# Two transformer blocks on one core: at five norms GpSimd adds the eighth chunk's squares, and TensorE's sums stand inside the second unit

## The chip, the cores and the metric

The kernel runs on one core of a Trainium2 chip. The metric is the device time of one execution in microseconds (us). The kernel before was timed three times: 914.53, 915.21 and 915.25 us, median 915.21 us.

## What is computed

Two stacked models run on 256 tokens of width 1024; the first adds 16 meta tokens in front, so most of its stages work on 272 columns. What matters here, cut from the reference:

```python
def rmsnorm(x, g):
    y = xf * lax.rsqrt(jnp.mean(xf * xf, axis=-1, keepdims=True) + NORM_EPS)
    return (y * g)

def conv_ffn(h, w_up, conv_w, conv_b, w_down):
    u = h @ w_up                       # 1024 -> 2 * 2816
    u = conv_b + sum(conv_w[j] * up[:, j:j + L] for j in range(3))
    gate, val = jnp.split(u, 2, axis=-1)
    return (jax.nn.silu(gate) * val) @ w_down

# first block, two layers: h += norm(mixer(norm(h))); h += norm(conv_ffn(norm(h)))
# second block: u = norm(h); proj = u @ w_in (gated linear attention and a convolution); h += mix @ w_out
#               u2 = norm(h); a, b = split(u2 @ w_gate_upffn); h += (silu(a) * b) @ w_down
#               u3 = norm(h); h += sigmoid(u3 @ w_ple_gate) * (p @ w_ple_proj); out = norm(h)
```

Every norm needs, for each token, the sum of 1024 squares before anything that was multiplied by it can be scaled.

## The kernel before, in words

Activations lie with their channels on the partitions: a tensor of 1024 channels is 8 chunks (DC = 8) of 128 channels x T tokens. All engine programs are written out by hand, one function for each engine (tensor, scalar, vector, gpsimd, and sync for the transfers), and meet through semaphores; each engine works its list in order. Nothing schedules them but the order in which the code stands.

**Weights.** A weight matrix is streamed in units. SP loads a unit into `raw`, ScalarE writes its rounded upper part `w_high`, VectorE (for some units with GpSimd, function `low`, L2031) writes the remainder `w_low` = raw - w_high. Two buffers of each alternate. TensorE makes three products for each 128x128 weight tile: high by high, low by high, high by low (L487 to L489, or L519, L520 and L525 where the first two are issued before the low part of the activation is there). An "up" unit has 16 tiles: 8 chunks of two blocks, so 48 products, each 256, 258 or 272 columns wide. The results of a unit stay in PSUM banks until VectorE takes them out, which also frees the banks; the unit after next uses the same banks.

**A norm.** The norm's gain is folded into the activation (`u_high`, `u_low`), and the factor 1/rms is applied to the results, since it is a factor of the token. So the first unit after a norm can be multiplied while the sum of squares is still being made. For the five norms of the change (named f0, f1, g, f2 and e: the three feed-forward "up" stages, the input projection of the second block, and the gate at the end) it goes like this:

- ScalarE writes `u_high` (L1094) and the squares of each chunk, into `m` (L1066, norms f0, f1, g) or into one of two buffers `sq` (L1076, norms f2 and e). VectorE writes `u_low` (L1455).
- GpSimd adds the squares of a chunk to `acc` (L2048, `add_square`), chunk after chunk, for chunks 0 to 6 (`range(DC - 1)`). For norms with squares in `m` it also waits for `u_low` of that chunk.
- TensorE multiplies the first unit, chunk after chunk as they come, and then issues `norm_sums`: for each of two or three token tiles a product of `acc` with a column of 1/1024 (L561), and the same for the squares of chunk 7 (L578, `last_sums`); both go into one PSUM bank. Each of these float32 products shows as two records in the trace.
- VectorE works nine small dependent steps on these sums (function `norm`, L1475 to L1493) and so has 1/rms of each token.
- TensorE spreads this over the partitions with `norm_rows` (L593), placed in the middle of the second unit: ahead of chunk 4 of 8.
- VectorE copies the rows (L1503) and from then on scales and takes out results (L1509).

At f0, f1 and g the second unit's `w_low` is made in two halves by VectorE at the very end of the stage before (L1546, `add_post`), after the last `u_low`. TensorE's second unit begins with a wait for the first half (`first_low`), and waits for the whole at chunk 4. At f2 and e it waits for the whole unit's parts at its start. At f2, GpSimd makes a quarter of each up unit's `w_low`.

The unit loop, where the change hangs its call (`between` is called ahead of the chunk of that number):

```python
                for at, k in enumerate(order or range(kc)):
                    ...
                    if middle is not None and at == kc // 2:
                        middle()
                    if first_low is not None and k * nb * P == first_half(n):
                        parts_ready(n)
                    if at in between:
                        between[at]()
```

Of the kernel before, what the change touches and what calls it, by code (L numbers as in the profile page):

```python
# [46 lines left out]
DC = D // P  # L47
# [35 lines left out]
BANKS = {"uv": UV_BANKS, "uk": UK_BANKS, "uqn": UQN_BANKS, "uqr": UQR_BANKS}  # L83
WO_BANKS = ((0, 2), (1, 3), (4, 5), (0, 2))
NORM_BANK, R_BANK = 6, 7

GUESS, GUESS_A, GUESS_B = 0x5F1FFFF9, 0.703952253, 2.38924456

# [131 lines left out]
def program(nc, dram, marks, final):  # L220
    ctx = ExitStack()
    with ctx:
# [8 lines left out]
        def done(name, i=None):  # L231


            engine, n, loop = marks.get(name, ("scalar", 1, None))
            stride = marks.get(("stride", engine, loop), 1)
            if final and name not in marks:
                raise KeyError(name)
            if isinstance(i, tuple):
                i, n = i[0], n - i[1] * stride
            return step_sems[engine], n if i is None else i * stride + n  # L240
# [24 lines left out]
        acc = sb("acc", [P, 2, 3 * P])  # L265
        sq = sb("sq", [P, 2, 3 * P])
# [200 lines left out]
        def _(pe):  # L467
# [26 lines left out]
            def unit(n, T, xs, chunk_ready=None, middle=None, i=None, order=None, first_low=None, between={}):  # L494

                U = UNITS[n]
                nb, kc = U["blocks"], U["tiles"] // U["blocks"]
                if first_low is not None:
                    pe.wait_ge(*done(first_low))
                elif n > 0:  # L500
                    parts_ready(n, i)
                for b in range(nb):
                    bank_free(U["first"] + b, i, 2 * nb)
                for at, k in enumerate(order or range(kc)):
                    high_ready, low_ready = chunk_ready if isinstance(chunk_ready, tuple) else (chunk_ready, None)
                    if high_ready is not None:
                        high_ready(k)
# [6 lines that stand above are left out]
                    out = [bank[BLOCKS[U["first"] + b]["bank"]][:, 0:T] for b in range(nb)]  # L514
                    if low_ready is not None:

                        for b in range(nb):
                            hi, lo = weights(n, k * nb + b)
                            nc.tensor.matmul(out[b], hi, xs[0][:, k, 0:T], start=at == 0, stop=False)  # L519
                            nc.tensor.matmul(out[b], lo, xs[0][:, k, 0:T], start=False, stop=False)  # L520
                        low_ready(k)
                    for b in range(nb):
                        hi, lo = weights(n, k * nb + b)
                        if low_ready is not None:
                            last = nc.tensor.matmul(out[b], hi, xs[1][:, k, 0:T], start=False, stop=at == kc - 1)  # L525
                        else:
                            last = three(out[b], hi, lo, xs[0][:, k, 0:T], xs[1][:, k, 0:T], at == 0, at == kc - 1)
                        if at == kc - 1:
                            last.then_inc(products, 1)
# [21 lines left out]
            def norm_sums(name, after, squares, last_chunk=False, over_what=None, late=(DC - 1,)):  # L551


                n, sums = len(squares), bank[NORM_BANK]
                what = over_what or [OVER_D] * n
                pe.wait_ge(*done(*after) if isinstance(after, tuple) else done(after))
                if over_what is not None:
                    nc.tensor.matmul(sums[:, 0:n], eps_w[:, :], ones[:, 0:n], start=True, stop=False,
                                     skip_group_check=True)
                for c, x in enumerate(squares):  # L560
                    last = nc.tensor.matmul(sums[0:x.shape[1], c:c + 1], x, over[:, what[c]:what[c] + 1],  # L561
                                            start=over_what is None and c == 0,
                                            stop=not last_chunk and c == n - 1, skip_group_check=True)
                for k in late if last_chunk else ():
                    if k == DC - 1:
                        last_sums(name, n)
                    else:
                        chunk_sums(name, n, k)
                if not last_chunk:
                    last.then_inc(*S.step(f"{name} sums"))  # L570
# [15 lines left out]
            def norm_rows(name, outs, first=0, signal=None):  # L586


                pe.wait_ge(*done(f"{name} inverse"))
                w = norm_height(name)  # L590
                for c, out in enumerate(outs):
                    unit_rows = ident if name in BY_SQRT else row_ident
                    last = nc.tensor.matmul(out, ny[0:w, first + c:first + c + 1].to_broadcast([w, P]),  # L593
                                            unit_rows[0:w, 0:out.shape[1]], start=True, stop=True)
                last.then_inc(*S.step(signal or f"{name} rows"))
# [25 lines left out]
            def token_rows(b, n, at=0):  # L621
                return [bank[b][:, at + t0:at + t0 + w] for t0, w in token_tiles(n)]
# [15 lines left out]
            def squares(a, n):  # L638
                return [acc[:, a, t0:t0 + w] for t0, w in token_tiles(n)]

            def ffn_up(l, T, sums_name):

                n0 = FIRST_UNIT[f"up{l}"]
                us = (uh, ul)
                unit(n0, T, us, high_then_low(sums_name))
                norm_sums(sums_name, f"{sums_name} acc {DC - 2}", squares(0, T), True)
                unit(n0 + 1, T, us, None, lambda: norm_rows(sums_name, token_rows(R_BANK, T)),
                     first_low=f"{sums_name} next low" if l < 2 else None)
                with pe.Fori(0, (FC - 2) // 2) as i:
                    for k in range(2):  # L650
                        unit(n0 + 2 + k, T, us, i=i)
# [296 lines left out]
            T = SEQ  # L948
            us = (uh, ul)
            unit(n, T, us, high_then_low("g"))  # L950
            norm_sums("g", f"g acc {DC - 2}", squares(0, T), True)
            unit(n + 1, T, us, None, lambda: norm_rows("g", token_rows(R_BANK, T)), first_low="g next low")
            pe.wait_ge(freed["v"], BLOCKS[FIRST_BLOCK["gin_a"]]["freed"])
            pe.wait_ge(tables_in, 16 * 6)
            for pair in range(2):
# [68 lines left out]
            ffn_down(2, T)  # L1024
            n = FIRST_UNIT["pgate"]
            unit(n, T, us, u_ready("e"))
            norm_sums("e", f"e acc {DC - 2}", squares(0, T), True)
            unit(n + 1, T, us, None, lambda: norm_rows("e", token_rows(R_BANK, T)))
            unit(n + 2, T, us)
            blocks_in_turn(n + 3, T, lambda b, k: (uh[:, k, 0:T], ul[:, k, 0:T]), DC,  # L1030
                           middle=lambda: norm_sums("out", f"out acc {DC - 5}", squares(0, T), True, late=()))
# [990 lines left out]
        def _(pool):  # L2022
# [16 lines left out]
            def add_square(name, c, T, ready, a=0, k=None):  # L2039
                label = c if k is None else k  # L2040
                pool.wait_ge(*ready)
                if name in SQUARES_IN_M and name != "out":

                    pool.wait_ge(*done(f"{name} u low {c}"))
                pool.wait_ge(*S.now())
                step = S.step(f"{name} acc {label}")
                x = m[:, c, 0:T] if name in SQUARES_IN_M else post1_square(c) if name == "post1" else sq[:, label % 2, 0:T]
                nc.gpsimd.tensor_tensor(acc[:, a, 0:T], acc[:, a, 0:T], x, ALU.add).then_inc(*step)  # L2048
# [35 lines left out]
                    add_square("post0", c, T1, done(f"post0 sq {c}"))  # L2084
                low(FIRST_UNIT["wo"] + u + 2)
            clear("post0")
            for c in range(DC - 1):
                add_square("f0", c, T1, done(f"f0 sq {c}"))
            up_lows(0)
            clear("f0")  # L2090
# [6 lines left out]
                add_square("post1", b, T1, done(f"post1 sq {b}"))  # L2097
            low(FIRST_UNIT["pool"] + 2)
            clear("post1")
            for c in range(DC - 1):  # L2100
                add_square("f1", c, SEQ + HISTORY, done(f"f1 sq {c}"))
            up_lows(1)
            clear("f1")
# [4 lines left out]
                nc.gpsimd.memset(t[:, :], 0.0).then_inc(*S.step())  # L2108
            nc.gpsimd.memset(Sd[:, :, :], 0.0).then_inc(*S.step("zeros"))
            clear("fpost1")  # L2110
            for c in range(DC - 1):
                add_square("g", c, T, done(f"g sq {c}"))
            for n in range(FIRST_UNIT["gin_a"] + 2, FIRST_UNIT["gin_c"] + 6):
                low(n)
            clear("g")
            for u in range(4):
                low(FIRST_UNIT["wout"] + u + 2)
                for c in range(2 * u, min(2 * u + 2, DC - 1)):
                    add_square("f2", c, T, done(f"f2 sq {c}"))
            low(FIRST_UNIT["pproj"] + 2)  # L2120
            up_lows(2)
# [7 lines left out]
                S.leave((DC - 2) // 2)  # L2129
            for c in range(DC - 2, DC):  # L2130
                low(n0 + c + 2)
                if c < DC - 1:
                    add_square("e", c, T, done(f"e sq {c}"))
            low(FIRST_UNIT["pgate"] + 2)
            low(FIRST_UNIT["pgate"] + 3)
            clear("e")
# [107 lines left out]
```

## Time and profile before

| | |
|---|---|
| median of 3 runs | 915.21 us (914.53 to 915.25) |
| the profiled execution's own time | 914.09 us |
| its span in the profile | 911.9 us |
| TensorE busy | 891.7 us, 98% of the span |
| VectorE busy | 680.7 us, 75% |
| ScalarE busy | 504.9 us, 55% |
| GpSimd busy | 180.9 us, 20% |
| chain that ended last | TensorE 87%, VectorE 7%, ScalarE 2% |
| mean granted TensorE clock | 0.994 |

The five norms stand at these times of the span: f0 at 143, f1 at 376, g at 577, f2 at 694 and e at 881 us. Their second units are where the timeline is to be read. A row of the timeline gives start, duration, engine, source line, operation, the tiles out<-in, and how many records are merged in it; in brackets stands idle time ahead of it and what ended it. Matmul records overlap each other, since they are pipelined: the pace is the distance between their starts.

### The profile page before, as it was taken

What the parts mean: (1) busy time and instruction counts of PE and PEld (TensorE: products, weight loads), DVE (VectorE), ACT (ScalarE), POOL (GpSimd) and SP (SyncE); (2) the same over time, 40 slices, a digit from 0 to 9 for tenths busy, and PEclk for the clock granted to TensorE, in tenths of its full rate; (3) what the DMA queues carried; (4) which work ended last, traced back from release to release, by engine and by line L of the source; (5) the groups of instructions that cost most, each with busy time, mean ns of one, the idle gap of its engine ahead of it and who ended that gap; (6) DMA issues with size and microseconds to landing.
All of it is one profiled execution on the core that took longest, in us unless ns stands there. A gap on an engine that the chain in (4) does not pass through costs nothing.

```text
span 911.9 us, 19861 instructions
## 1 busy us (share of the span) xinstructions
PE 891.7 (98%) x7330; PEld 868.3 (95%) x7330; DVE 680.7 (75%) x1174; ACT 504.9 (55%) x843; POOL 180.9 (20%) x165
## 2 busy tenths in 40 slices
PE   8999999999999998999999999999999999999997
PEld 8987889999999998999999999999999999999996
DVE  7767539999995427999999544889887888875556
ACT  6677656666664345666666535654465444444443
POOL 0029751000000014200000003100034333313312
PEclk9999999999999999999999999999999999999998
DMA  6652133544464530355555554333354555564431
GB/s 231 191 134 94 48 139 139 181 174 160 176 232 156 215 137 10 130 184 184 184 184 206 174 206 154 133 145 140 139 177 159 189 187 187 190 237 178 169 139 47
DMA packets 25731, 146.81 MB, mean 161 GB/s; under 512 B 3008, under 2 KB 9168, under 8 KB 10448
## 3 DMA queue, kind: packets, MB, share of 16 engines
q1 hardware_dynamic: 25680, 146.11, 45.4%
q8 instruction: 34, 0.56, 0.3%
q14 instruction: 17, 0.14, 0.0%
HBM read 142.82 MB, written 1.05 MB: 158 GB/s over the span
## 4 chain that ended last, share of the span: by engine, by line
PE 87%; DVE 7%; ACT 2%; DMA 1%; issue 1%; POOL 1%; SPq 0%; DVEq 0%; ACTq 0%; POOLq 0%
PE bank L487 25%; PE bank L488 25%; PE bank L489 24%; PE bank L746 2%; DVE u_low L1455 1%; PE bank L941 1%; DVE h L1535 1%; PE bank L762 1%; DVE bank L1527 1%; PE bank L593 1%; PE bank L780 1%; PE bank L578 1%; PE bank L525 1%; ACT w_high L1058 1%; DMA raw<-w_dq_dram 1%
## 5 line engine op out<-in xcount | busy, mean ns | idle before, releaser
L487 PE MATMUL bank<-u_high,w_high 128*128 128x256 f32 (+2 forms) x1328 | 379.2, 286 | 3.1 <-ACT m L1066 1.2
L488 PE MATMUL bank<-u_low,w_high 128*128 128x256 f32 (+2 forms) x1328 | 377.0, 284 | 0.0
L489 PE MATMUL bank<-u_high,w_low 128*128 128x256 f32 (+2 forms) x1328 | 375.8, 283 | 0.0
L1446 DVE TENSOR_TENSOR w_low<-raw,w_high 128x1024 fp32r<-128x1024 f32 (+6 forms) x112 | 190.7, 1702 | 101.6 <-ACT w_high L1058 100.5
L487 PEld LDWEIGHTS bank<-u_high,w_high 128*128 128x128 f32 x1328 | 250.8, 189 | 5.4 <-issue 1.3
L488 PEld LDWEIGHTS bank<-u_low,w_high 128*128 128x128 f32 x1328 | 250.4, 189 | 0.0
L489 PEld LDWEIGHTS bank<-u_high,w_low 128*128 128x128 f32 x1328 | 250.2, 188 | 0.0
L1058 ACT ACTIVATE w_high<-raw 128x1024 fp32r<-128x1024 f32 (+6 forms) x119 | 189.5, 1592 | 67.8 <-PE bank L489 60.4
L487 PE MATMUL bank<-x_high,w_high 128*128 128x256 f32 (+1 forms) x608 | 172.2, 283 | 0.3 <-DVE x_low L1886 0.3
L489 PE MATMUL bank<-x_high,w_low 128*128 128x256 f32 (+1 forms) x608 | 172.5, 284 | 0.0
L488 PE MATMUL bank<-x_low,w_high 128*128 128x256 f32 (+1 forms) x608 | 171.8, 283 | 0.0
L2048 POOL TENSOR_TENSOR acc<-acc,sq 128x256 f32<-128x256 f32 (+1 forms) x32 | 42.7, 1333 | 487.7 <-ACT sq L1076 486.7
L487 PEld LDWEIGHTS bank<-x_high,w_high 128*128 128x128 f32 x608 | 114.6, 188 | 0.7 <-issue 0.7
L488 PEld LDWEIGHTS bank<-x_low,w_high 128*128 128x128 f32 x608 | 114.5, 188 | 0.0
L489 PEld LDWEIGHTS bank<-x_high,w_low 128*128 128x128 f32 x608 | 114.3, 188 | 0.0
L1055 ACT ACTIVATE w_high<-raw 128x1024 fp32r<-128x1024 f32 (+2 forms) x68 | 69.6, 1023 | 71.1 <-PE bank L489 67.2
L2031 POOL TENSOR_TENSOR w_low<-raw,w_high 128x512 fp32r<-128x512 f32 (+1 forms) x29 | 64.3, 2216 | 140.4 <-ACT w_high L1058 140.4
L1440 DVE TENSOR_TENSOR w_low<-raw,w_high 128x1024 fp32r<-128x1024 f32 (+2 forms) x68 | 80.2, 1179 | 13.0 <-ACT w_high L1055 10.9
L1595 DVE SCALAR_TENSOR_TENSOR conv_out<-conv_in,par,conv_out 128x272 f32<-128x272 f32 (+1 forms) x176 | 79.1, 489 | 7.6 <-ACT conv_out L1128 2.0
L1509 DVE TENSOR_TENSOR conv_in<-bank,r_rows 128x256 f32<-128x256 f32 (+2 forms) x140 | 54.2, 427 | 15.7 <-PE bank L489 10.3
L1135 ACT ACTIVATE conv_out<-conv_out 128x272 f32<-128x272 f32 (+1 forms) x44 | 18.7, 425 | 73.7 <-DVE conv_out L1595 73.7
L1128 ACT ACTIVATE conv_out<-conv_in,par 128x272 f32<-128x272 f32 (+1 forms) x88 | 48.2, 595 | 9.6 <-DVE conv_in L1509 9.2
(236 smaller groups left out, 1101.3 us busy)
## 6 DMA issues: line engine op xcount, KB each, us to landing
raw<-w_up_dram SPq DMA_DIRECT2D x66, 1024.0 KB, 4.8
raw<-w_down_dram SPq DMA_DIRECT2D x24, 1408.0 KB, 6.0
raw<-w_gin_c_dram SPq DMA_DIRECT2D x4, 1536.0 KB, 6.6
raw<-w_wo_dram SPq DMA_DIRECT2D x4, 1024.0 KB, 5.6
raw<-w_wout_dram SPq DMA_DIRECT2D x4, 1024.0 KB, 4.9
raw<-w_pgate_dram SPq DMA_DIRECT2D x4, 1024.0 KB, 4.8
raw<-w_gin_v_dram SPq DMA_DIRECT2D x2, 1024.0 KB, 5.0
raw<-w_gin_g_dram SPq DMA_DIRECT2D x2, 1024.0 KB, 4.8
```

What stands on the lines that cost most here:

```text
L487: nc.tensor.matmul(out, hi, rhi, start=start, stop=False)
L488: nc.tensor.matmul(out, hi, rlo, start=False, stop=False)
L489: return nc.tensor.matmul(out, lo, rhi, start=False, stop=stop)
L1055: nc.scalar.activation(wh[n % 2][:, 0:split], raw[n % 2][:, 0:split], ACT.Copy).then_inc(*S.step(first))
L1058: nc.scalar.activation(wh[n % 2][:, split:cols], raw[n % 2][:, split:cols], ACT.Copy).then_inc(high_parts, 1)
L1128: nc.scalar.activation(cv[:, hf, 0:T], ur[:, hf, 2 + skip:2 + skip + T], ACT.Identity, bias=pcol(f"cb{l}", hf * FC + j), scale=pcol(f"cw{l ...
L1440: nc.vector.tensor_tensor(wl[n % 2][:, 0:split], raw[n % 2][:, 0:split], wh[n % 2][:, 0:split].bitcast(F32), ALU.subtract)\
L1446: nc.vector.tensor_tensor(wl[n % 2][:, split:cols], raw[n % 2][:, split:cols], wh[n % 2][:, split:cols].bitcast(F32), ALU.subtract).then_i ...
L1509: nc.vector.tensor_tensor(out, bank[BLOCKS[b]["bank"]][:, 0:T], rows[:, 0:T], ALU.mult)\
L1595: nc.vector.scalar_tensor_tensor(cv[:, hf, 0:T], ur[:, hf, skip + tap:skip + tap + T], pcol(f"cw{l}", (tap * 2 + hf) * FC + j), cv[:, hf, ...
L2031: nc.gpsimd.tensor_tensor(wl[n % 2][:, at], raw[n % 2][:, at], wh[n % 2][:, at].bitcast(F32), ALU.subtract).then_inc(low_parts_g, pool_cou ...
L2048: nc.gpsimd.tensor_tensor(acc[:, a, 0:T], acc[:, a, 0:T], x, ALU.add).then_inc(*step)
```

## The change

At the five norms GpSimd adds the squares of all eight chunks into `acc`. TensorE no longer multiplies the squares of chunk 7 by themselves; `norm_sums` is one group of two or three products, of `acc` alone. It moves from behind the first unit to the inside of the second, ahead of its third chunk (`SUMS_AT = 2`). It waits for GpSimd's eighth add. `norm_rows` stays ahead of the fifth chunk of the same unit. VectorE's and ScalarE's lists are unchanged.

```diff
+SUMS_AT = 2
...
                 unit(n0, T, us, high_then_low(sums_name))
-                norm_sums(sums_name, f"{sums_name} acc {DC - 2}", squares(0, T), True)
                 unit(n0 + 1, T, us, None, lambda: norm_rows(sums_name, token_rows(R_BANK, T)),
+                     between={SUMS_AT: lambda: norm_sums(sums_name, f"{sums_name} acc {DC - 1}", squares(0, T))},
                      first_low=f"{sums_name} next low" if l < 2 else None)
...
             unit(n, T, us, high_then_low("g"))
-            norm_sums("g", f"g acc {DC - 2}", squares(0, T), True)
-            unit(n + 1, T, us, None, lambda: norm_rows("g", token_rows(R_BANK, T)), first_low="g next low")
+            unit(n + 1, T, us, None, lambda: norm_rows("g", token_rows(R_BANK, T)), first_low="g next low",
+                 between={SUMS_AT: lambda: norm_sums("g", f"g acc {DC - 1}", squares(0, T))})
...
             unit(n, T, us, u_ready("e"))
-            norm_sums("e", f"e acc {DC - 2}", squares(0, T), True)
-            unit(n + 1, T, us, None, lambda: norm_rows("e", token_rows(R_BANK, T)))
+            unit(n + 1, T, us, None, lambda: norm_rows("e", token_rows(R_BANK, T)),
+                 between={SUMS_AT: lambda: norm_sums("e", f"e acc {DC - 1}", squares(0, T))})
...
-            for c in range(DC - 1):
+            for c in range(DC):
                 add_square("f0", c, T1, done(f"f0 sq {c}"))
...
-            for c in range(DC - 1):
+            for c in range(DC):
                 add_square("f1", c, SEQ + HISTORY, done(f"f1 sq {c}"))
...
-            for c in range(DC - 1):
+            for c in range(DC):
                 add_square("g", c, T, done(f"g sq {c}"))
...
                 low(FIRST_UNIT["wout"] + u + 2)
-                for c in range(2 * u, min(2 * u + 2, DC - 1)):
+                for c in range(2 * u, 2 * u + 2):
                     add_square("f2", c, T, done(f"f2 sq {c}"))
...
                 low(n0 + c + 2)
-                if c < DC - 1:
-                    add_square("e", c, T, done(f"e sq {c}"))
+                add_square("e", c, T, done(f"e sq {c}"))
```

On TensorE, norm f0, from the end of the first unit (L520 and L525) into the second (L487 to L489); before:

```order
L525 MATMUL bank<-u_low,w_high 128x272 x2
L561 MATMUL bank<-mean_weights,acc 91x1 x3
L578 MATMUL bank<-mean_weights,m 91x1 x3
L487 MATMUL bank<-u_high,w_high 128x272
L488 MATMUL bank<-u_low,w_high 128x272
L489 MATMUL bank<-u_high,w_low 128x272
```

And the change at the same place (its lines are numbered one higher), from the end of the second chunk of the second unit on, where the sums now stand:

```order
L488 MATMUL bank<-u_high,w_high 128x272
L489 MATMUL bank<-u_low,w_high 128x272
L490 MATMUL bank<-u_high,w_low 128x272
L562 MATMUL bank<-mean_weights,acc 91x1 x3
L488 MATMUL bank<-u_high,w_high 128x272
L489 MATMUL bank<-u_low,w_high 128x272
L490 MATMUL bank<-u_high,w_low 128x272
```

Twelve products of the second unit now stand ahead of the sums and twelve between them and the rows (L593, now L594), where 24 stood between sums and rows; the group on `m` is gone.

On GpSimd, norm f2, ahead of its share of the up units' `w_low`; before:

```order
L2031 TENSOR_TENSOR w_low<-raw,w_high 128x512
L2048 TENSOR_TENSOR acc<-acc,sq 128x256
L2031 TENSOR_TENSOR w_low<-raw,w_high 128x512
```

And in the change:

```order
L2032 TENSOR_TENSOR w_low<-raw,w_high 128x512
L2049 TENSOR_TENSOR acc<-acc,sq 128x256 x2
L2032 TENSOR_TENSOR w_low<-raw,w_high 128x512
```

One more add stands ahead of GpSimd's next share of `w_low`.

## Rows read from the trace of the kernel before

**Rows 1.** The page, part 1: busy time, share of the span, instructions.

```profile
PE 891.7 (98%) x7330; PEld 868.3 (95%) x7330; DVE 680.7 (75%) x1174; ACT 504.9 (55%) x843; POOL 180.9 (20%) x165
```

**Rows 2.** Timeline, TensorE, norm f0; columns as told in the section on the profile.

```profile
142.65 0.62 PE L578 MATMUL bank<-mean_weights,m 128*91 128x1 f32 x6
143.23 0.39 PE L487 MATMUL bank<-u_high,w_high 128*128 128x272 f32 x1
...
144.84 0.28 PE L487 MATMUL bank<-u_high,w_high 128*128 128x272 f32 x1
...
146.34 0.80 PE L593 MATMUL bank<-row_ident,norm_y 91*128 91x91 f32 x6
```

**Rows 3.** Timeline, VectorE, norm f0: first half of w_low, norm steps, taking out.

```profile
141.38 1.79 DVE L1546 TENSOR_TENSOR w_low<-raw,w_high 128x1024 fp32r<-128x1024 f32 x1
...
144.23 0.14 DVE L1475 TENSOR_SCALAR norm_t<-bank 91x3 int32<-91x3 int32 x1
...
145.76 0.16 DVE L1493 SCALAR_TENSOR_TENSOR norm_y<-norm_t,norm_y 91x3 f32<-91x3 f32 x1
...
148.63 0.79 DVE L1509 TENSOR_TENSOR conv_in<-bank,r_rows 128x272 f32<-128x272 f32 x2
```

**Rows 4.** Timeline, GpSimd, norm f0: the seventh add.

```profile
141.18 0.91 POOL L2048 TENSOR_TENSOR acc<-acc,m 128x272 f32<-128x272 f32 x1 [0.44 <-ACT m L1066]
```

**Rows 5.** Timeline, norm f1: second half of w_low, second unit's start, rows.

```profile
376.50 1.21 DVE L1546 TENSOR_TENSOR w_low<-raw,w_high 128x1024 fp32r<-128x1024 f32 x1
376.63 0.39 PE L487 MATMUL bank<-u_high,w_high 128*128 128x258 f32 x1
...
379.62 0.80 PE L593 MATMUL bank<-row_ident,norm_y 86*128 86x86 f32 x6
```

**Rows 6.** Timeline, norm g: first half of w_low, second unit's start, rows.

```profile
575.20 1.76 DVE L1546 TENSOR_TENSOR w_low<-raw,w_high 128x1024 fp32r<-128x1024 f32 x1
...
577.26 0.37 PE L487 MATMUL bank<-u_high,w_high 128*128 128x256 f32 x1
...
580.18 0.60 PE L593 MATMUL bank<-row_ident,norm_y 128*128 128x128 f32 x4
```

**Rows 7.** Timeline, norm f2: TensorE, VectorE's steps, GpSimd's share of w_low.

```profile
693.24 0.50 PE L561 MATMUL bank<-mean_weights,acc 128*128 128x1 f32 x4
693.60 0.58 PE L578 MATMUL bank<-mean_weights,sq 128*128 128x1 f32 x4
694.05 0.36 PE L487 MATMUL bank<-u_high,w_high 128*128 128x256 f32 x1
...
694.22 0.16 DVE L1475 TENSOR_SCALAR norm_t<-bank 128x2 int32<-128x2 int32 x1 [2.45 <-PE bank L578]
...
695.58 1.30 POOL L2031 TENSOR_TENSOR w_low<-raw,w_high 128x512 fp32r<-128x512 f32 x1 [2.66 <-ACT w_high L1058]
...
695.60 1.30 DVE L1491 SCALAR_TENSOR_TENSOR norm_t<-norm_t 128x2 f32<-128x2 f32 x1
...
697.15 0.71 PE L593 MATMUL bank<-row_ident,norm_y 128*128 128x128 f32 x4
```

**Rows 8.** Timeline, norm e: u_low of chunks 6 and 7, chunk 7, rows.

```profile
872.04 0.96 DVE L1455 SCALAR_TENSOR_TENSOR u_low<-h,par,u_high 128x256 fp32r<-128x256 f32 x1
...
879.84 0.48 DVE L1455 SCALAR_TENSOR_TENSOR u_low<-h,par,u_high 128x256 fp32r<-128x256 f32 x1
...
880.47 0.36 PE L487 MATMUL bank<-u_high,w_high 128*128 128x256 f32 x1
...
884.98 0.60 PE L593 MATMUL bank<-row_ident,norm_y 128*128 128x128 f32 x4
```

**Rows 9.** By source line, 668 to 671 us: two adds beside two u_low (min/median/max ns).

```profile
L2048 POOL TENSOR_TENSOR acc<-acc,sq x2: 742/1442/2143, 667.9 to 670.2; 128x256 f32<-128x256 f32 x2
...
L1455 DVE SCALAR_TENSOR_TENSOR u_low<-h,par,u_high x2: 958/963/968, 669.3 to 670.2; 128x256 fp32r<-128x256 f32 x2
```

**Rows 10.** TensorE in one stretch: length, busy, granted clock, DMA share, GB/s.

```profile
360.00:370.00 10.00, 8.55 (x59) 0.83 0.32 107
```

## The prediction

> **What bounds the kernel now.** I read the page first, for the shares: TensorE is busy for 98% of the span, VectorE for 75%, GpSimd for 20% [rows 1]. So a change pays only if it takes time from TensorE's list without making TensorE wait, and every new wait of TensorE is paid in full. Next I read the timeline at each of the five norms, TensorE beside VectorE and GpSimd. The reader is to see three things there.
>
> First, at f0 and f1 the second unit does not start when the sums are done but when the first half of its `w_low` is there. At f0 VectorE's first half runs from 141.38 for 1.79 us, to 143.17, and TensorE's first product stands at 143.23 [rows 2, 3]. At f1 the second half starts as the first ends, near 376.55, and TensorE starts at 376.63 [rows 5]. At g the first half ends at 576.96 and TensorE starts at 577.26, so there the sums held it [rows 6].
>
> Second, between sums and rows there are two chains side by side. TensorE's own 24 products take 3.11 us at f0 (143.23 to 146.34), 2.99 at f1 and 2.92 at g [rows 2, 5, 6]. VectorE's nine steps take 1.69 us at f0 (144.23 to 145.76 plus 0.16) [rows 3]; at f2 they take 2.87 us, of which 1.14 is one step that took 1.30 instead of 0.16, so 1.73 undisturbed [rows 7]. To this come 0.17 us from the first product behind the sums to the first step (694.05 to 694.22) and 0.06 from the last step (ending at 697.09) to the rows (697.15) [rows 7]. Today the 24 products cover this chain everywhere but at f2, where TensorE waits 0.2 us (24 products would end at 696.97).
>
> Third, VectorE and GpSimd take turns when both read SBUF. The first half at f0 takes 1.79 us where the same work takes 1.21 [rows 3, 5]; GpSimd's seventh add began just before it, at 141.18 [rows 4], and 141.18 + 1.21 + an add of some 0.77 is 143.16, the end seen. So they ran one after the other. At f2 the 1.30 us step starts 0.02 us behind a GpSimd `w_low` of 1.30 us and ends with it [rows 7].
>
> **What the change removes.** One group of small products at each norm: 0.36 us where it has four records (693.24 to 693.60) [rows 7]; with six I take 0.43 in proportion to the whole groups below. Together 2 x 0.43 + 3 x 0.36 = 1.94 us off TensorE's list. It is not all gained, since the unit that follows is held at f0, f1 and nearly at g.
>
> **What it adds and moves.** The remaining group costs 0.58 us with six records (142.65 to 143.23) and 0.45 with four (693.60 to 694.05) [rows 2, 7]. The group that is removed gives the lower bound, 0.43 and 0.36; I take the upper, because these are the rows in which TensorE goes from the sums back into a unit, as it now does. Behind the sums stand 12 products instead of 24: about 1.5 us. The chain needs 0.17 + 1.69 or 1.73 + 0.06 = 1.92 or 1.96 us. So TensorE waits about 0.45 us at the rows of every norm, whatever else happens. This is the core of the forecast: the wait alone eats what the removed group saves. Now each place.
>
> *f0.* The second unit still cannot start before 143.23. Twelve products end at 144.84 [rows 2]. GpSimd's eighth add can start when the seventh is through (142.09 by rows 4), finds VectorE in the first half, runs behind it until about 143.9 and pushes the second half to about 145.0; both are ready in time. Sums: 144.84 + 0.58 + 0.17 = 145.59 for the first step, rows at 145.59 + 1.69 + 0.06 = 147.34 instead of 146.34: **+1.00**.
>
> *f1.* 376.63 + 1.55 (half of 2.99, and 0.05 since the first half of such a run is the slower one) + 0.58 + 0.17 + 1.69 + 0.06 = 380.68 instead of 379.62: **+1.06**.
>
> *g.* The unit starts at 576.96 + 0.06 = 577.02. Then 1.51 + 0.45 + 0.17 + 1.73 + 0.06 gives 580.94 instead of 580.18: **+0.76** [rows 6].
>
> *f2.* Weights and squares are there early; the eighth add runs at about 688, in an idle time of VectorE, ahead of GpSimd's next `w_low`. The unit starts at 693.24, where the removed group stood. 1.41 (24 products without their slower start, halved) + 0.45 + 0.17: first step at 695.27, third step, the first that reads SBUF twice, at 695.66. But GpSimd's `w_low` runs from 695.58 to 696.88 [rows 7], triggered by ScalarE's work on the next weights, which does not move. Today it meets the eighth step; now it meets the third, which ends at 696.90, and six more steps of 0.195 end at 698.07. Rows at 698.13 instead of 697.15: **+0.98**. If they miss each other the rows stand at 697.08, 0.07 earlier; I take the meeting, because the third or, at the latest, the fifth step falls into those 1.30 us.
>
> *e.* The eighth add is new beside `u_low` of chunk 7. For chunk 6 there is an add, and its `u_low` takes 0.96 us; for chunk 7 there is none, and it takes 0.48 [rows 8]. TensorE takes up chunk 7 at 880.47, right behind this `u_low` (880.32). So chunk 7 comes 0.48 later. Then, from the end of the first unit, 1.41 + 0.45 + 0.17 + 1.73 + 0.06 = 3.82 us to the rows, where now 0.81 + 2.92 = 3.73 pass: **+0.57**. If the add does not get in, +0.09.
>
> The sum is 1.00 + 1.06 + 0.76 + 0.98 + 0.57 = **4.37 us**. Behind the rows everything is the same work. VectorE's list shifts a little more than TensorE's at f0 (its last step from 145.92 to 147.28, 1.36 against 1.00); it then has to take out the first unit's results, today until 149.42 [rows 3], before the third unit can start near 150.0 (the rows' 0.6 and 24 products of 3.1 after 146.34). That margin of 0.6 shrinks to 0.2 and holds. Nothing later waits for anything but TensorE's progress, so I let the 4.37 pass through. The profiled execution took 914.09 us, 1.12 less than the median; 914.09 + 4.37 = 918.46, and against the median 915.21 + 4.37 = **919.6 us**.
>
> **A rule against the row.** Who wins when the eighth add and the waiting first half meet? The row: of two adds in a row beside two waiting `u_low`, the first add held off the first `u_low`, then that `u_low` ran (969 ns until 670.3), and the second add, from 670.2, held off the second [rows 9]. They alternate, so at f0 the first half keeps its end at 143.17. The Trainium skill ("SBUF — State Buffer", section "Who interferes with whom") says that a VectorE instruction with two SBUF inputs and a GpSimd instruction that reads SBUF exclude each other for a whole instruction, and that issue order decides. By that rule too the first half, issued at 141.38, goes ahead of the add; if instead the add were counted first, the first rival below would be the sum. The same rule speaks against the change as such: it puts five more GpSimd instructions beside VectorE's most urgent work.
>
> **Rivals.** *The add goes first.* GpSimd's eighth add follows its seventh at once and VectorE's first half waits for both. The first half at f0, f1 and g then ends about 0.75 us later (1.79 - 1.21 = 0.58 was the part of one add that it met; a whole undisturbed one is 742 ns [rows 9]), and TensorE's second unit with it: + 2.25, in all 6.6 us, 921.8. For it: the first half shows that a GpSimd instruction in flight is never broken off. Against it: rows 9. Chance 0.10.
>
> *The clock falls.* At f2 TensorE will wait some 1.6 us (from 695.10 + 1.41 to 698.13). The one stretch in mid-span where the granted clock is below 1 follows a wait and small sums of similar size: 8.55 us busy in 10, granted 0.83 [rows 10], which is 1.7 us lost at the lower of the two levels (1.2 GHz). That would give 6.1 us, 921.3. Against it: at f2 twelve full products lie between sums and wait. Chance 0.05.
>
> *The chain fits (not slower).* If rows were never waited for, because the sums reach VectorE sooner than 0.17 us or its steps run closer, what is left is TensorE's own list: at f0 and f1, where the start is held anyway, +0.58 each; at g -0.24 + 0.45; at f2 and e -0.36 each. That is +0.65 us, 915.9. It decides at a chain of 1.5 us from sums to rows, against 1.92 in the rows. Against it: nine dependent steps at a distance of 0.19 have one length. Chance 0.07. If beyond that the first halves did not hold the second unit, the whole 1.94 us would be gained, 913.3; chance 0.03.
>
> **How the numbers follow.** A measurement of this kernel can tell about 0.2%, 1.8 us, from no change. My forecast, 0.75, with its bounds: sums at their lower costs -0.57, f2 without the meeting -1.05, e without the collision -0.48, which leaves 2.27 us and 917.5. That is still over 0.2%. Upwards the rivals of the add and of the clock reach 921.8. So the range is 917.5 to 921.9, faster 0.03, within 0.2% 0.07, slower 0.90.
>
> **What would show it.** TensorE idle ahead of the rows at all five norms, released by VectorE's last step: about 0.45 us at four, 1.6 at f2. The second unit of f0 and f1 starting as long after the last `u_low` as today. The second half of `w_low` at f0, f1 and g taking 1.9 instead of 1.21 us (if it is the first half that grows, the first rival holds). `u_low` of chunk 7 at e taking 0.96. I am wrong if the rows are reached without a wait, or if the time is under 917.

## The result, and the profile after

The changed kernel takes 918.78 us (median of 6 runs, 917.84 to 919.36) against 915.11 us before (6 runs). The ratio is 1.0044, with a 95% interval of 1.0034 to 1.0054: slower by some 4 us. The forecast was 919.6 us.

The page's first part of the kernel after:

```profile
PE 891.4 (97%) x7306; PEld 866.8 (95%) x7306; DVE 682.6 (74%) x1174; ACT 504.7 (55%) x843; POOL 188.3 (21%) x170
```

The 24 records fewer on TensorE (12 products in two records each) took nothing off its busy time that one would see, and the span grew from 911.9 to 916.4 us. So the time went into waits: TensorE's idle time grew from 20.2 to 25.0 us. The first two rows of TensorE's waits in the kernel after, longest in total first (columns: us in total, times, longest); the lines are numbered one higher than before:

```profile
PE bank L594 <- DVE norm_y L1494: 2.1, 5, 1.1
PE bank L488 <- DVE w_low L1547: 2.1, 3, 0.9
```

Neither row was in the list before. The first is the wait for VectorE's last norm step, at all five norms. The second is the wait for the first half of `w_low` at f0, f1 and g, which the sums had covered.

**Where the time went, norm by norm.** The same few waits of TensorE occur in both traces between the norms, so their starts serve as marks. Timeline of the kernel before (the fence holds TensorE's rows; ScalarE's `u_high` of chunk 7 at e, the mark between f2 and e, has a fence of its own):

```profile
141.11 0.51 PE L525 MATMUL bank<-u_low,w_high 128*128 128x272 f32 x2 [0.19 <-DVE u_low L1455]
341.69 0.33 PE L865 MATMUL bank<-w_high,u_high 128*96 128x256 f32 x1 [0.36 <-ACT u_high L1094]
374.55 0.51 PE L525 MATMUL bank<-u_low,w_high 128*128 128x258 f32 x2 [0.17 <-DVE u_low L1455]
566.88 0.36 PE L519 MATMUL bank<-u_high,w_high 128*128 128x256 f32 x1 [0.22 <-ACT u_high L1094]
664.13 0.36 PE L487 MATMUL bank<-x_high,w_high 128*128 128x256 f32 x1 [0.30 <-DVE x_low L1886]
903.28 0.77 PE L578 MATMUL bank<-mean_weights,m 128*128 128x1 f32 x4 [0.69 <-ACT m L1066]
```

```profile
877.51 0.49 ACT L1094 ACTIVATE u_high<-h,par 128x256 fp32r<-128x256 f32 x1
```

The same marks in the kernel after:

```profile
140.80 0.52 PE L526 MATMUL bank<-u_low,w_high 128*128 128x272 f32 x2 [0.20 <-DVE u_low L1456]
342.38 0.33 PE L866 MATMUL bank<-w_high,u_high 128*96 128x256 f32 x1 [0.36 <-ACT u_high L1095]
376.46 0.51 PE L526 MATMUL bank<-u_low,w_high 128*128 128x258 f32 x2 [0.18 <-DVE u_low L1456]
569.83 0.36 PE L520 MATMUL bank<-u_high,w_high 128*128 128x256 f32 x1 [0.22 <-ACT u_high L1095]
667.86 0.36 PE L488 MATMUL bank<-x_high,w_high 128*128 128x256 f32 x1 [0.29 <-DVE x_low L1887]
908.16 0.61 PE L579 MATMUL bank<-mean_weights,m 128*128 128x1 f32 x4 [0.69 <-ACT m L1067]
```

```profile
881.79 0.49 ACT L1095 ACTIVATE u_high<-h,par 128x256 fp32r<-128x256 f32 x1
```

After minus before, from mark to mark: f0 (-0.31 to +0.69) is +1.00 us; f1 (+1.91 to +2.95) +1.04; g (to +3.73) +0.78; f2 (to +4.28) +0.55; e (to +4.88) +0.60. Together **3.97 us**. Between f0 and f1 the trace after lost another 1.22 us, from +0.69 to +1.91. It is left out of the sum; the last section says what is known of it.

**Norm f0 in the kernel after.** TensorE, then VectorE, then GpSimd (the two halves of `w_low` in rows of their own):

```profile
142.93 0.39 PE L488 MATMUL bank<-u_high,w_high 128*128 128x272 f32 x1 [0.87 <-DVE w_low L1547]
...
144.53 0.57 PE L562 MATMUL bank<-mean_weights,acc 128*91 128x1 f32 x6
144.96 0.37 PE L488 MATMUL bank<-u_high,w_high 128*128 128x272 f32 x1
...
146.91 0.90 PE L594 MATMUL bank<-row_ident,norm_y 91*128 91x91 f32 x6 [0.19 <-DVE norm_y L1494]
147.60 0.38 PE L488 MATMUL bank<-u_high,w_high 128*128 128x272 f32 x1
```

```profile
141.09 1.79 DVE L1547 TENSOR_TENSOR w_low<-raw,w_high 128x1024 fp32r<-128x1024 f32 x1
142.80 1.78 DVE L1547 TENSOR_TENSOR w_low<-raw,w_high 128x1024 fp32r<-128x1024 f32 x1
...
145.14 0.16 DVE L1476 TENSOR_SCALAR norm_t<-bank 91x3 int32<-91x3 int32 x1 [0.56 <-PE bank L562]
...
146.70 0.16 DVE L1494 SCALAR_TENSOR_TENSOR norm_y<-norm_t,norm_y 91x3 f32<-91x3 f32 x1
```

```profile
140.88 0.91 POOL L2049 TENSOR_TENSOR acc<-acc,m 128x272 f32<-128x272 f32 x1 [0.43 <-ACT m L1067]
141.96 1.53 POOL L2049 TENSOR_TENSOR acc<-acc,m 128x272 f32<-128x272 f32 x1 [0.17 <-POOL acc L2049]
```

The unit starts 1.84 us after the first half began, as before (143.23 - 141.38 = 1.85, [rows 2, 3]): it was held by that half then, and it is now, only that now the trace shows the wait of 0.87 us. The first half keeps its 1.79 us; the second takes 1.78 us, where 1.21 stood before [rows 5]. The eighth add, issued at 141.96, lasts 1.53 us, twice its usual 0.77: it lets the first half finish, and the second half waits for it. VectorE's first step comes 0.61 us behind the start of the sums, the last ends at 146.86, and the rows follow at once. The group of rows then takes 0.69 us to the next product (146.91 to 147.60), where it took 0.59 before:

```profile
146.93 0.37 PE L487 MATMUL bank<-u_high,w_high 128*128 128x272 f32 x1
```

### The profile page after: what moved, and what is told of

Same layout as the page of the kernel before. It is cut to its first block, busy times and chain, and to the rows that moved or that the text cites. A ratio compares the mean times of both kernels' runs of the same rounds, so it can differ in the third digit from the quotient of the medians.

```text
span 916.4 us, 19823 instructions
## 1 busy us (share of the span) xinstructions
PE 891.4 (97%) x7306; PEld 866.8 (95%) x7306; DVE 682.6 (74%) x1174; ACT 504.7 (55%) x843; POOL 188.3 (21%) x170
## 4 chain that ended last, share of the span: by engine, by line
PE 84%; DVE 11%; ACT 2%; issue 1%; DMA 1%; POOL 1%; SPq 0%; DVEq 0%; POOLq 0%; ACTq 0%
PE bank L488 24%; PE bank L489 24%; PE bank L490 24%; DVE u_low L1456 2%; PE bank L747 2%; DVE h L1536 1%; DVE bank L1528 1%; PE bank L594 1%; PE bank L942 1%; PE bank L763 1%; DVE w_low L1447 1%; PE bank L781 1%; ACT w_high L1059 1%; PE bank L562 1%; PE bank L579 1%
## 5 line engine op out<-in xcount | busy, mean ns | idle before, releaser
L489 PE MATMUL bank<-u_low,w_high 128*128 128x256 f32 (+2 forms) x1328 | 377.1, 284 | 0.0
L489 PEld LDWEIGHTS bank<-u_low,w_high 128*128 128x128 f32 x1328 | 250.5, 189 | 0.0
L489 PE MATMUL bank<-x_low,w_high 128*128 128x256 f32 (+1 forms) x608 | 171.8, 283 | 0.0
L2049 POOL TENSOR_TENSOR acc<-acc,sq 128x256 f32<-128x256 f32 (+1 forms) x34 | 45.5, 1338 | 490.4 <-ACT sq L1077 489.2
L489 PEld LDWEIGHTS bank<-x_low,w_high 128*128 128x128 f32 x608 | 114.5, 188 | 0.0
```

The lines of the kernel that those rows point to most:

```text
L489: nc.tensor.matmul(out, hi, rlo, start=False, stop=False)
```

## The experiments

Theory 1 is the forecast's: the place of the sums costs, since 12 products do not cover VectorE's steps, and the saved group is worth nothing where the unit waits for `w_low`. Theory 2: GpSimd's five added adds cost, by holding VectorE. Theory 3: a longer stretch of low clock makes part of the difference. For each kernel the ratio of its time to the kernel before's is given, and the shifts at the five norms against the profile before, from mark to mark as above (one profile of each kernel, read to 0.01 us).

| kernel | f0 | f1 | g | f2 | e | sum | ratio, 95% interval |
|---|---|---|---|---|---|---|---|
| the change | +1.00 | +1.04 | +0.78 | +0.55 | +0.60 | +3.97 | 1.0044 (1.0034 to 1.0054) |
| sums ahead of the second chunk | +0.51 | +0.49 | +0.26 | -0.05 | +0.02 | +1.23 | 1.0011 (1.0002 to 1.0021) |
| place only | +1.49 | +1.49 | +1.28 | +1.13 | +0.55 | +5.94 | 1.0066 (1.0050 to 1.0081) |
| adds only | +1.14 | +1.10 | +0.82 | -0.55 | +0.01 | +2.52 | 1.0047 (1.0031 to 1.0063) |
| rows two chunks later | +0.86 | +1.04 | +3.19 | +0.51 | +0.58 | +6.18 | 1.0048 (1.0032 to 1.0064) |
| late add at e | +1.00 | +1.01 | +0.81 | +0.55 | +0.11 | +3.48 | 1.0045 (1.0028 to 1.0062) |
| f2 and e only | +0.04 | -0.01 | 0.00 | -0.55 | -0.42 | -0.94 | 0.9996 (0.9987 to 1.0005) |

### The sums one chunk earlier

```diff
-SUMS_AT = 2
+SUMS_AT = 1
```

> The change with the sums one chunk earlier in the second unit (ahead of its second chunk instead of its third). Theory 1 (the place costs: with 12 products between sums and rows VectorE's nine steps are not covered): 18 products, some 2.2 us, cover 1.95 us, so TensorE has no wait at the rows at f0, f1, g and e, at most 0.1 at f2. What is left against before: f0 and f1 +0.5 each (the unit is held by the first half of w_low, and the group now stands behind it), g +0.2, f2 0, e +0.1 (u_low +0.48, group -0.36). Sum +1.3 to +1.5 us, 916.5 us. Theory 2 (the five added GpSimd adds cost, by holding VectorE): they are all still there, so nothing is won, 918.5 to 919. Theory 3 (part of the difference is the longer stretch of low clock between f0 and f1, not the norms): the norms' sum in the trace is then unlike the time's difference.

Measured: 915.82 us (median of 11 runs) beside 914.96. Norm f0 on TensorE in this kernel:

```profile
142.98 0.39 PE L488 MATMUL bank<-u_high,w_high 128*128 128x272 f32 x1 [0.86 <-DVE w_low L1547]
...
143.84 0.57 PE L562 MATMUL bank<-mean_weights,acc 128*91 128x1 f32 x6
...
146.59 0.80 PE L594 MATMUL bank<-row_ident,norm_y 91*128 91x91 f32 x6
```

There is no wait ahead of the rows at four norms. At f2 there are 0.48 us, where at most 0.1 was expected: VectorE's eighth step still meets GpSimd's `w_low` and takes 1.04 instead of 0.16 us. All five adds are there, and so is the wait for the first half; what is left at f0 is 0.51 us: the group that now stands behind that wait (0.43, from 143.84 to the next product at 144.27) and the slower start of that product. One chunk more between sums and rows brings back 2.7 of the 4.0 us. Theory 2 expected nothing to come back.

### The place alone

```diff
-            for c in range(DC):
+            for c in range(DC - 1):
                 add_square("f0", c, T1, done(f"f0 sq {c}"))
...
-                     between={SUMS_AT: lambda: norm_sums(sums_name, f"{sums_name} acc {DC - 1}", squares(0, T))},
+                     between={SUMS_AT: lambda: norm_sums(sums_name, f"{sums_name} acc {DC - 2}", squares(0, T), True)},
```

(against the change, and so at all five norms)

> The place alone: seven adds and both groups as before, moved together ahead of the third chunk of the second unit. Theory 1: rows later by 1.5 us at f0 and f1, 1.1 at g, 1.0 at f2, 0.5 at e (no new add beside u_low, so that one stays at 0.48 us). Sum +5.1 us, 920.2 us; TensorE waits about 0.45 us ahead of the rows at four norms. Theory 2: without the adds there is no loss; below 916.5 us. In both the second half of w_low at f0, f1 and g is back at 1.21 us.

Measured: 920.9 us. Without a single added add the kernel is slower than the change. So theory 2 falls as the account of the loss; what the adds cost at single places, two experiments below tell. In the trace the second half of `w_low` at f0 is back at its own duration, and so is `u_low` of chunk 7 at e:

```profile
143.02 1.21 DVE L1547 TENSOR_TENSOR w_low<-raw,w_high 128x1024 fp32r<-128x1024 f32 x1
```

```profile
885.66 0.48 DVE L1456 SCALAR_TENSOR_TENSOR u_low<-h,par,u_high 128x256 fp32r<-128x256 f32 x1
```

The difference to the change at f0, 0.49 us, is the second group, now in the path of the sums. Place by place 1.5, 1.5, 1.1, 1.0 and 0.5 us were expected and 1.49, 1.49, 1.28, 1.13 and 0.55 found. (The places expected add up to 5.6; the 5.1 given with them was added wrongly.)

### The adds alone

```diff
                 unit(n0, T, us, high_then_low(sums_name))
-                norm_sums(sums_name, f"{sums_name} acc {DC - 2}", squares(0, T), True)
+                norm_sums(sums_name, f"{sums_name} acc {DC - 1}", squares(0, T))
```

(against the kernel before, at all five norms, with GpSimd's list as in the change)

> The adds alone: eight adds, one group of sums, but behind the first unit, where the sums were before. Theory 1: no wait ahead of the rows anywhere (24 products in between), but TensorE waits for the eighth add at f0, f1 and g, since that runs behind the first half of w_low: +1.0, +1.1, +0.7 us. At f2 the group is saved and VectorE's steps end before GpSimd's w_low starts: -0.5. At e +0.1. Sum +2.4 us, 917.5 us. Theory 2 expects about as much as the change, +3.7 us, 918.8, since all five adds are there.

Measured: 918.54 us from 4 runs that lie far apart (916.38 to 920.95); the profiled one is the fastest. Theory 1 expected 917.5 and theory 2 918.8, so the time alone does not tell them apart; the norms in the trace do. They give +2.52 us. The interval of the ratio does not reach down to that; the other runs lost more than the profiled one, and their granted clock was lower (0.989 in the slowest, 0.994 in the profiled). The last 1.0 us between 917.5 and 918.54 has no cause shown. The norms themselves came as expected: 1.14, 1.10 and 0.82 us at f0, f1 and g (1.0, 1.1 and 0.7 expected), -0.55 at f2 and nothing at e, and no wait ahead of the rows anywhere. At f0 TensorE and GpSimd:

```profile
143.76 0.64 PE L561 MATMUL bank<-mean_weights,acc 128*91 128x1 f32 x6 [1.48 <-POOL acc L2048]
```

```profile
142.17 1.53 POOL L2048 TENSOR_TENSOR acc<-acc,m 128x272 f32<-128x272 f32 x1 [0.17 <-POOL acc L2048]
```

So the adds do cost at f0, f1 and g when TensorE needs the sum right behind the first unit: the eighth add stands behind VectorE's first half. The change had hidden this cost inside the second unit and paid for hiding it.

### The rows two chunks later

```diff
-SUMS_AT = 2
+SUMS_AT, ROWS_AT = 2, 6
...
-                unit(n0 + 1, T, us, None, lambda: norm_rows(sums_name, token_rows(R_BANK, T)),
-                     between={SUMS_AT: lambda: norm_sums(sums_name, f"{sums_name} acc {DC - 1}", squares(0, T))},
+                unit(n0 + 1, T, us,
+                     between={SUMS_AT: lambda: norm_sums(sums_name, f"{sums_name} acc {DC - 1}", squares(0, T)),
+                              ROWS_AT: lambda: norm_rows(sums_name, token_rows(R_BANK, T))},
```

> The change, with the rows two chunks later too (ahead of the seventh chunk), so that again 24 products lie between sums and rows. Theory 1: TensorE's waits ahead of the rows (0.2 to 1.1 us each) go, but VectorE can take out the first unit's results only later, and the third unit needs their banks: the wait moves to the start of the third unit at f1 (0.5), e (0.6) and f2 (0.9), f0 0.2. Net 0.5 to 1.5 us won of the 3.7: 917.3 to 918.3. If VectorE's work behind the rows had room, all of it would be won back: 915.5 to 916. Theory 2: unchanged, 918.8.

Measured: 919.81 us. That is outside what I expected: it lost, instead of winning 0.5 to 1.5. The waits ahead of the rows are gone. At f1, f2 and e they are back at the third unit, as expected, with 0.16, 0.73 and 0.44 us, now for VectorE's taking out; f0 shows no idle time there, but its product comes 0.19 us late. So nothing is won at f1, f2 and e, and 0.14 us at f0. The surprise is g. TensorE there, and VectorE:

```profile
589.01 0.55 PE L972 MATMUL bank<-w_high,u_high 128*128 128x256 f32 x1 [1.40 <-issue]
```

```profile
585.17 0.42 DVE L1507 COPY r_rows<-bank 128x256 f32<-128x256 f32 x1 [1.43 <-PE bank L594]
585.63 0.42 DVE L1513 TENSOR_TENSOR gate_low_rank<-bank,r_rows 128x256 f32<-128x256 f32 x1
585.97 0.74 DVE L1812 SCALAR_TENSOR_TENSOR gla_q<-bank,r_rows 128x256 f32<-128x256 f32 x2
586.63 2.28 DVE L1450 TENSOR_TENSOR w_low<-raw,w_high 128x2048 fp32r<-128x2048 f32 x1
```

At g VectorE stands idle for 1.43 us until the rows come, and the next unit's `w_low` is queued behind the three operations that use them. It ends at 588.91, and TensorE starts on it at 589.01. I had looked at the banks only. Besides, the clock fell behind this wait (TensorE by stretch: length, busy, granted clock, DMA share, GB/s):

```profile
585.00:590.00 5.00, 3.60 (x22) 0.89 0.16 48
590.00:595.00 5.00, 5.00 (x35) 0.77 0.65 218
```

5 x 0.11 + 5 x 0.23 = 1.7 us. With the wait of 1.40 that is nearly all of the 3.19 at g.

### The late add at e

```diff
+                if c == DC - 1:
+                    pool.wait_ge(*done(f"e u low {c}"))
                 add_square("e", c, T, done(f"e sq {c}"))
```

> The change, with GpSimd's eighth add at e waiting also for VectorE's u_low of chunk 7. The lock theory: u_low of chunk 7 is back from 0.96 to 0.48 us, the add runs after it beside an idle VectorE and ends before TensorE wants it, so 0.48 us of the 0.59 at e come back; the other four norms as in the change. 918.2 us. If the 0.48 us at e had another cause, nothing changes.

Measured: 919.18 us with 915.85 to 919.89, against 918.2 expected; 0.48 us is below what these runs can tell. The trace tells it: at e +0.11 us instead of +0.60, and the other four norms as in the change. `u_low` of chunk 7 and GpSimd's eighth add in this kernel:

```profile
884.96 0.48 DVE L1456 SCALAR_TENSOR_TENSOR u_low<-h,par,u_high 128x256 fp32r<-128x256 f32 x1
```

```profile
885.52 0.73 POOL L2049 TENSOR_TENSOR acc<-acc,sq 128x256 f32<-128x256 f32 x1 [7.68 <-DVE u_low L1456]
```

In the change the same two took 0.96 and 2.13 us:

```profile
884.13 0.96 DVE L1456 SCALAR_TENSOR_TENSOR u_low<-h,par,u_high 128x256 fp32r<-128x256 f32 x1
```

```profile
882.67 2.13 POOL L2049 TENSOR_TENSOR acc<-acc,sq 128x256 f32<-128x256 f32 x1 [5.66 <-ACT sq L1077]
```

Nothing but the add's start differs, so the 0.48 us were the meeting of the two.

### At f2 and e alone

```diff
                 unit(n0, T, us, high_then_low(sums_name))
-                norm_sums(sums_name, f"{sums_name} acc {DC - 2}", squares(0, T), True)
+                if l < 2:
+                    norm_sums(sums_name, f"{sums_name} acc {DC - 2}", squares(0, T), True)
+                else:
+                    norm_sums(sums_name, f"{sums_name} acc {DC - 1}", squares(0, T))
...
-            norm_sums("e", f"e acc {DC - 2}", squares(0, T), True)
+            norm_sums("e", f"e acc {DC - 1}", squares(0, T))
...
-                for c in range(2 * u, min(2 * u + 2, DC - 1)):
+                for c in range(2 * u, 2 * u + 2):
...
-                if c < DC - 1:
-                    add_square("e", c, T, done(f"e sq {c}"))
+                if c == DC - 1:
+                    pool.wait_ge(*done(f"e u low {c}"))
+                add_square("e", c, T, done(f"e sq {c}"))
```

(against the kernel before)

> The kernel before, with the eighth add and a single group of sums behind the first unit at f2 and e alone, where the adds-only run lost nothing, and e's add after u_low of chunk 7; f0, f1 and g as before. The chain theory: at f2 the group is saved and the norm steps end before GpSimd's w_low begins, -0.54 us as in the adds-only run; at e -0.36 us. Sum -0.9 us, 914.1 us beside 915.0: faster than both, by less than 0.2%. If saved groups were worth nothing: 915.0.

Measured: 914.25 us (median of 12 runs) beside 914.62. The trace gives -0.94 us at the two norms. The interval, 0.9987 to 1.0005, holds both this and no change at all: the traces show the gain at the two norms, and no run shows that the kernel as a whole is faster. Norm f2 on TensorE:

```profile
693.20 0.50 PE L561 MATMUL bank<-mean_weights,acc 128*128 128x1 f32 x4
...
696.46 0.61 PE L593 MATMUL bank<-row_ident,norm_y 128*128 128x128 f32 x4
```

From sums to rows 3.26 us, where 3.91 were before [rows 7]: one group of 0.36 us, and no meeting with GpSimd's `w_low`, since VectorE's last step now ends at 695.46 and that starts at 695.54.

## Why the prediction was right, and where its sum was off

Sign, size and mechanism hold: 4.37 us were forecast, the five norms gave 3.97 in the trace, and the ratio's interval means 3.1 to 4.9 us. But three terms of the sum were off, and they partly cancel: the sums were taken too dear at all five norms, a cost of the rows was left out, and f2 met GpSimd later than said.

- **The second unit is held by the first half at f0, f1 and g.** Right: waits of 0.87, 0.85 and 0.40 us for it are in the trace after. With the sums ahead of the second chunk, where nothing else is left, f0 and f1 still lose 0.5 us each, the group of sums that stood in this wait before.
- **Twelve products do not cover nine steps.** Right, and this is the largest part: 18 products do at four norms, and 2.7 us come back. From the start of the last product to the rows, less one product's 0.12 us, TensorE lost 0.36, 0.44, 0.46 and 0.46 us at f0, f1, g and e, where 0.45 was forecast; the profile counts only 0.19 to 0.30 of it as idle.
- **f0, f1, g.** +1.00, +1.06, +0.76 forecast; 1.00, 1.04, 0.78 found. That these agree to 0.02 us is luck. The forecast was of the place of the rows, and measured from the mark ahead of the norm they came only 0.88, 0.93 and 0.68 us later (f0: 146.91 + 0.31 - 146.34). The sums cost 0.43, 0.41 and 0.36 us up to the next product, not 0.58, 0.58 and 0.45: the lower of the two costs. The other 0.1 us stands behind: the group of rows took 0.59, 0.58 and 0.36 us up to the next product before, and 0.69, 0.69 and 0.46 now, a term that the forecast put at nothing. With the rows two chunks later, where TensorE does not wait for them, it is 0.59, 0.59 and 0.36 again. The eighth add let the first half finish and held the second, as forecast.
- **f2.** +0.98 forecast, 0.55 found. This is the term that was mis-sized most. The step that failed is "first step at 695.27, third step at 695.66", behind the start of GpSimd's `w_low`. The group of sums took 0.36 us here too (698.36 to 698.72), not 0.45. So the third step just got in ahead and the fifth one met GpSimd:

```profile
699.30 0.16 DVE L1482 TENSOR_TENSOR norm_t<-norm_y 128x2 f32<-128x2 f32 x1
...
699.68 0.94 DVE L1486 SCALAR_TENSOR_TENSOR norm_y<-norm_t,norm_y 128x2 f32<-128x2 f32 x1
```

```profile
699.31 1.31 POOL L2032 TENSOR_TENSOR w_low<-raw,w_high 128x512 fp32r<-128x512 f32 x1 [2.65 <-ACT w_high L1059]
```

The third step started 0.01 us ahead of GpSimd, the fourth, which takes one of its inputs from a bank, ran beside it in 0.16 us, and the fifth was held; two steps of 0.195 fewer remained behind it, which is the 0.4 us. The forecast had named the fifth step as the latest possible and taken the earliest. Counted as above, TensorE lost 1.23 us ahead of the rows instead of 1.6 (1.07 in the profile). That the third is the first step that GpSimd can hold was wrong as well: with the place alone it held the second (last section).
- **e.** +0.57 forecast, 0.60 found, by the same two errors: the rows came 0.49 us later, and their group takes 0.46 instead of 0.36. 0.48 of it is the meeting at chunk 7, by an experiment of its own.
- **Everything behind the rows passes through.** Right for the change. The rows two chunks later show how little room there was: VectorE's work behind the rows, not only the banks, then holds TensorE.
- **The rival of the clock.** It did not come at f2: the granted clock stayed at 1.00 behind the wait of 1.07 us, and behind 1.21 us there with the place alone. Behind the wait at g with the rows two chunks later it did fall.
- **The rival on the other side** (the chain fits, +0.65 us) was the right arithmetic for another kernel: with the sums ahead of the second chunk the chain does fit at four norms, and with the meetings at f2 and e it gives +1.23.

## What to carry to other kernels

A signal that another engine must turn round has to be placed by the length of that turn. Count the work between the question and the answer against the other engine's steps before moving the question later: here about 0.4 us of products saved at each of five places cost more than that in cover. Work that stands in a wait is free, and taking it away gains nothing (f0 and f1 here). And when a sum agrees at one place to 0.02 us, look whether each of its terms does. And when an operation is given to GpSimd, look at which VectorE operation it will stand beside, at that very place; the same add cost 0.48 us or nothing, by when it was released.

## What the runs showed of the hardware that I had not expected

**The clock's low stretch differs from profile to profile.** Between f0 and f1 the granted clock falls behind a wait of TensorE of about 1.24 us in every trace. (With the adds alone TensorE waits 1.48 us at f0 and 1.43 at f1, and the clock stays at 1.00 there.) Before (columns: length, then busy time with count of TensorE, its weight loads, VectorE, ScalarE and GpSimd, granted clock, DMA share, GB/s):

```profile
364.00:366.00 2.00, 2.00 (x13) 2.00 (x12) 1.21 (x3) 1.43 (x2) 0.00 (x0) 0.57 0.85 324
366.00:368.00 2.00, 2.00 (x12) 2.00 (x12) 1.74 (x6) 1.40 (x5) 0.75 (x1) 0.58 0.41 164
368.00:370.00 2.00, 1.80 (x13) 1.38 (x12) 2.00 (x6) 1.59 (x4) 0.79 (x2) 1.00 0.00 0
```

After:

```profile
364.00:366.00 2.00, 2.00 (x10) 2.00 (x11) 0.17 (x1) 1.66 (x2) 0.33 (x1) 0.50 0.84 238
366.00:368.00 2.00, 2.00 (x10) 2.00 (x10) 1.24 (x3) 0.69 (x2) 0.00 (x0) 0.50 0.69 291
368.00:370.00 2.00, 2.00 (x11) 2.00 (x10) 1.79 (x5) 1.40 (x5) 0.75 (x1) 0.51 0.03 8
```

By five-microsecond stretches the low clock costs 1.7 us in the traces of before, of place only, of adds only and of f2 and e only, and 3.4 or 3.5 us in those of the change, the sums ahead of the second chunk, the late add and, at this place, the rows two chunks later. Place only has the short stretch and the largest ratio of all, so theory 3 does not explain the change's loss. The long stretch goes with more time lost between the marks of f0 and f1 (1.22, 1.11, 1.64 and 0.89 us in these four), but not by its length alone: place only and adds only lose 0.50 and 0.42 there with the short one, and f2 and e only nothing. The four profiles with the long stretch are those of the kernels that have both the eight adds and the moved sums. From one profile each it can't be told whether that is chance; against it, the norms' 3.97 us alone already exceed the 3.67 between the medians. The kernel before varies by itself: beside the last two experiments its 17 runs lie between 913.35 us (granted clock 0.995) and 916.4 (0.990). What sets the length was not tried.

**Which step of VectorE GpSimd holds.** At f2 in the change a step issued 0.01 us ahead of GpSimd's start was not held, and the next one, which reads PSUM and one SBUF tile, ran undisturbed beside it. The one after, with both inputs in SBUF, waited until the end (0.94 instead of 0.16 us). The Trainium skill ("SBUF — State Buffer", section "Who interferes with whom") says that a VectorE instruction with two SBUF inputs contends with a GpSimd instruction that reads SBUF, and that one with at most one SBUF input does so only in the modes in which it takes both ports; on the first the trace agrees. Two inputs are not needed, though: with the place alone the second step, a TENSOR_SCALAR with one SBUF input, was issued 0.23 us behind GpSimd's start and held for 1.09 us. That fits the second half of the sentence, if the step ran in such a mode, which the trace does not show:

```profile
700.48 1.09 DVE L1479 TENSOR_SCALAR norm_y<-norm_t 128x2 int32<-128x2 int32 x1
```

```profile
700.25 1.30 POOL L2032 TENSOR_TENSOR w_low<-raw,w_high 128x512 fp32r<-128x512 f32 x1 [2.65 <-ACT w_high L1059]
```
